# Attention values in float32r: probabilities in two parts, value tiles of 128 stationary columns

## The reference

```python
x = layer_norm(ALPHA * x + 0.5 * swiglu(x, ffn1...))
x = layer_norm(ALPHA * x + hybrid_mixer(x, ...))
x = layer_norm(ALPHA * x + memory_cross_attention(x, mem, ...))
x = layer_norm(ALPHA * x + 0.5 * swiglu(x, ffn2...))
```

```python
o_s = swa_sink_attention(q_s, k_s, v_s, sinks)      # 8 heads of 64, 2 key/value heads, window of 128 keys, a sink per head
o_f = forgetting_attention(q_f, k_f, v_f, f_logit)  # "FoX": 8 heads of 64, causal, with a cumulative forget gate
merged = gates[:, :, 0] * (o_s @ w_branch_swa) + gates[:, :, 1] * (o_f @ w_branch_fox)
return merged @ w_out
```

## Time and profile before

| | |
|---|---|
| median of 3 runs | 1303.44 us (1303.38 to 1303.83) |
| the profiled execution | 1306.2 us, span 1304.4 us |
| PE busy | 1268.3 us, 97% |
| DVE busy | 715.5 us, 55% |
| ACT busy | 449.2 us, 34% |
| POOL busy | 90.4 us, 7% |
| granted TensorE clock | 0.992 of full speed over the span |
| chain that ended last | PE 91%, DVE 3%, POOL 2%, DMA 1%, ACT 1% |

### The profile page before, as it was taken

One profiled execution on the slowest core, in us unless ns is written; L12 is line 12 of the kernel. 1 busy time (PEld: TensorE's weight loads), 2 busy tenths in 40 slices (PEclk: granted clock), 3 DMA queues, 4 the chain that ended last, 5 costly groups with the idle time before them and its releaser, 6 DMA issues.

```text
span 1304.4 us, 16284 instructions
## 1 busy us (share of the span) xinstructions
PE 1268.3 (97%) x6065; PEld 1050.1 (81%) x6065; DVE 715.5 (55%) x994; ACT 449.2 (34%) x699; POOL 90.4 (7%) x126
## 2 busy tenths in 40 slices
PE   7999999999998999999999999999999999999995
PEld 6888888888887887877778887888888888888884
DVE  4644444444475666565644557554664444444446
ACT  3322222222245654455533325342422222222221
POOL 2000000000032100001010030002300000000004
PEclk9999999999999999999999999999999999999998
DMA  7433333333327222222163205213343333333311
GB/s 228 144 96 96 96 96 96 96 96 96 96 66 211 81 82 71 59 56 59 49 209 98 96 33 177 82 49 97 97 129 96 96 96 96 96 96 96 96 48 65
DMA packets 163129, 128.03 MB, mean 98 GB/s; under 512 B 5120, under 2 KB 150544, under 8 KB 163088
## 3 DMA queue, kind: packets, MB, share of 16 engines
q1 hardware_dynamic: 159872, 116.44, 29.8%
q0 software_dynamic: 3008, 11.01, 2.4%
q10 hardware_dynamic: 208, 0.01, 0.0%
HBM read 123.25 MB, written 4.19 MB: 98 GB/s over the span
## 4 chain that ended last, share of the span: by engine, by line
PE 91%; DVE 3%; POOL 2%; DMA 1%; ACT 1%; issue 1%; SPq 0%; DVEq 0%; POOLq 0%; ACTq 0%
PE bank L601 19%; PE bank L603 19%; PE bank L602 19%; PE banks_scores L601 9%; PE banks_scores L603 9%; PE banks_scores L602 9%; PE bank L880 2%; PE bank L862 1%; DVE ring_lo L1406 1%; PE banks_scores L832 1%; PE banks_scores L831 1%; DVE stats L1438 1%; PE bank L619 1%; DMA raw<-in_ffn_w_gate 1%; DVE xT_lo L1406 1%
## 5 line engine op out<-in xcount | busy, mean ns | idle before, releaser
L1406 DVE TENSOR_TENSOR ring_lo<-raw,ring_hi 128x1024 fp32r<-128x1024 f32 x215 | 261.0, 1234 | 123.6 <-ACT ring_hi L1090 123.3
L601 PE MATMUL bank<-xT_hi,ring_hi 128*128 128x512 f32 (+1 forms) x728 | 280.6, 385 | 4.5 <-DVE ring_lo L1406 2.3
L1090 ACT ACTIVATE ring_hi<-raw 128x1024 fp32r<-128x1024 f32 x215 | 221.7, 1056 | 176.5 <-DMA raw<-in_ffn_w_up 89.4
L602 PE MATMUL bank<-xT_lo,ring_hi 128*128 128x512 f32 (+1 forms) x728 | 278.4, 382 | 0.0
L603 PE MATMUL bank<-xT_hi,ring_lo 128*128 128x512 f32 (+1 forms) x728 | 278.3, 382 | 0.0
L601 PEld LDWEIGHTS bank<-xT_hi,ring_hi 128*128 128x128 f32 x728 | 138.8, 191 | 31.0 <-issue 3.9
L603 PEld LDWEIGHTS bank<-xT_hi,ring_lo 128*128 128x128 f32 x728 | 138.7, 191 | 26.3
L602 PEld LDWEIGHTS bank<-xT_lo,ring_hi 128*128 128x128 f32 x728 | 138.9, 191 | 24.9
L601 PE MATMUL banks_scores<-xT_hi,ring_hi 128*128 128x512 f32 (+1 forms) x368 | 140.7, 382 | 0.0
L602 PE MATMUL banks_scores<-xT_lo,ring_hi 128*128 128x512 f32 (+1 forms) x368 | 140.3, 381 | 0.0
L603 PE MATMUL banks_scores<-xT_hi,ring_lo 128*128 128x512 f32 (+1 forms) x368 | 140.3, 381 | 0.0
(11 more groups left out here) (274 smaller groups left out, 1783.0 us busy)
## 6 DMA issues: line engine op xcount, KB each, us to landing
raw<-in_ffn_w_gate SPq DMA_DIRECT2D x44, 512.0 KB, 4.7
raw<-in_ffn_w_up SPq DMA_DIRECT2D x44, 512.0 KB, 4.4
raw<-in_ffn_w_down SPq DMA_DIRECT2D x44, 512.0 KB, 3.3
raw<-in_mix_w_in SPq DMA_DIRECT2D x34, 512.0 KB, 3.8
raw<-in_mem_w_k SPq DMA_DIRECT2D x8, 512.0 KB, 4.1
raw<-in_mix_w_out SPq DMA_DIRECT2D x8, 512.0 KB, 3.2
raw<-in_mem_w_v SPq DMA_DIRECT2D x8, 512.0 KB, 3.2
raw<-in_mem_w_q SPq DMA_DIRECT2D x8, 512.0 KB, 4.7
```

Of the source, the lines that this page charges most:

```text
L601: pe.matmul(dst, hi, mhi, start=start, stop=False)
L602: pe.matmul(dst, hi, mlo, start=False, stop=False)
L1090: nc.scalar.activation(dst, src, copy).then_inc(unit_hi, 1)
L1406: nc.vector.tensor_tensor(dst, src, hi.bitcast(F32), ALU.subtract).then_inc(done, 1)
```

## The change

1. The values product is made of two float32r passes per tile, on the high and on the low part of the transposed probabilities (`probT_hi`, `probT_lo`). The stationary tile holds 128 columns: high and low values side by side. So rows 0 to 63 of bank 7 hold the product with one part of the values and rows 64 to 127 that with the other, and the head's output is the sum of the two halves.
2. ScalarE moves the other half into `o_other` (`output_other`), VectorE adds it to the own half into `os_sum` or `of_sum` (`output_sum`), one head each. The next head's values wait for that sum (`o_added`). The pair's parts are now taken from the sums, at the end of an odd turn.
3. `copied_probs` is done for every bank by both engines: high part by ScalarE, low part by VectorE, and the bank is free after the low part.
4. The tiles of windowed and FoX values are split in the same way (`value_parts_high`, `value_parts_low`), with the order high, low, high for a windowed head and high, low, low, high for a pair of FoX heads, so that either head of a pair finds its own order.
5. From unit 74 (`U_F`) to unit 116 the ring has four slots; two of the six lend their memory to `probT_lo` and to half of the FoX values. `prep(n)` waits for the last user of its slot, unit n - 4. Units 74 and 75 take the slots of 72 and 73.

The diff, cut to its core:

```diff
+MIX_RING = 4
+def slot(n):
+    return (n - U_F) % MIX_RING if U_F <= n < U_OUT else n % RING
+def slot_user(n):
+    for m in range(n - 1, -1, -1):
+        if slot(m) == slot(n):
+            return m
+    return None
...
         def _(pe):
-                if H % 2 == 0 and H >= 2:
-                    pe.wait_ge(o_lo, H // 2)
-                dst = ps[7][HD * (H % 2):HD * (H % 2 + 1), :]
+                if H >= 1:
+                    pe.wait_ge(o_added, H)
                 for k in range(TB):
                     if H < SWA_HEADS:
-                        v = vs[:, k, HD * (H // 4):HD * (H // 4 + 1)]
+                        v = vs_parts[:, k, H // 4, H % 2:H % 2 + 2, :]
...
-                        v = vf[:, k, HD * h:HD * (h + 1)]
+                        v = vf_parts[h // 4][:, k, h // 2 % 2, 2 * (h % 2):2 * (h % 2) + 2, :]
...
-                    mm = pe.matmul(dst[:, P * k:end], v, probT[:, src:src + end - P * k], start=k == 0, stop=k == TB - 1,
+                    pe.matmul(bank(7)[:, P * k:end], v, probT_hi[:, cols], start=k == 0, stop=False, skip_group_check=True)
+                    mm = pe.matmul(bank(7)[:, P * k:end], v, probT_lo[:, cols], start=False, stop=k == TB - 1,
                                    skip_group_check=True)
...
         def _(act):
-                    if n >= RING:
-                        act.wait_ge(unit_used, n - RING + 1)
+                    if slot_user(n) is not None:
+                        act.wait_ge(unit_used, slot_user(n) + 1)
...
             for m in range(4):
+                if m == 1:
+                    value_parts_high(vs_parts, T_VS, ((every, every, every, 0), (every, every, every, 2)))
                 prep(U_QS + m + 4)
...
             def copied_probs(H):
                 for e, n in enumerate(head_uses(H)):
-                    if e != 1:
+                    act.wait_ge(t_full, n + 1)
+                    w = probs_width(H, e)
+                    high(probT_hi[:, HALF * e:HALF * e + w], bank(5 + n % 2)[:, 0:w], probs_hi)
+            def output_other(H):
+                act.wait_ge(o_full, H + 1)
+                if H >= 1:
+                    act.wait_ge(o_added, H)
+                own, other = rows_of(H)
+                nc.scalar.activation(o_other[own, :], ps[7][other, :], copy).then_inc(o_moved, 1)
...
             for H in range(HEADS):
+                if H == SWA_HEADS + 1:
+                    output_other(H - 2)
+                    pair_high((H - 3) // 2)
                 for i, u in enumerate(fill(H % 8)):
-                    if i == 1 and 3 <= H != SWA_HEADS + 1:
-                        pair_high(H - 2)
...
+                if H >= 2 and H != SWA_HEADS + 1:
+                    output_other(H - 2)
                 if H >= 1:
                     copied_probs(H - 1)
-                if H == SWA_HEADS:
-                    pair_high(H - 1)
+                if H < SWA_HEADS:
+                    for u in fill(H):
+                        if u >= 8:
+                            value_parts_high(vf_parts[(u - 8) // 2][:, :, (u - 8) % 2], T_VF[u - 8], ((every, every, slice(0, 4, 3)),))
                 exponentials(...)
                 if H + 1 < HEADS:
                     stack_high(H + 1)
+                if H >= 3 and H % 2 and H != SWA_HEADS + 1:
+                    pair_high((H - 3) // 2)
...
                 if u == 0:
+                    output_other(HEADS - 2)
                     copied_probs(HEADS - 1)
-                    pair_high(HEADS - 1)
+                    output_other(HEADS - 1)
+                    pair_high(HEADS // 2 - 1)
...
         def _(dve):
+            def copied_probs(H, banks=range(2)):
+                for e in banks:
+                    n, w = head_uses(H)[e], probs_width(H, e)
+                    cols = slice(HALF * e, HALF * e + w)
+                    copied[0] += 1
+                    dve.wait_ge(probs_hi, copied[0])
+                    low(probT_lo[:, cols], bank(5 + n % 2)[:, 0:w], probT_hi[:, cols], t_free[n % 2])
+            def output_sum(H):
+                own, _ = rows_of(H)
+                m = H // 2
+                dve.wait_ge(o_moved, H + 1)
+                nc.vector.tensor_tensor((os_sum if m < 4 else of_sum)[own, m % 4, :], ps[7][own, :], o_other[own, :], ALU.add)\
+                    .then_inc(o_added, 1)
```

More of the change, by code:

```diff
@@ L218, in program @@
         qf = place("qf", [P, 4, SEQ], F32, z_q)
-        vf = place("vf", [P, TB, FOX_HEADS * HD], F32, z_v)
+        vf_parts = [place(f"vf_parts{i}", [P, TB, 2, 4, HD], F32R, at) for i, at in enumerate((z_v, z_hi_end))]
         vm_hi = place("vm_hi", [P, MB, D], F32R, z_v)
@@ L1233, in _, with value_parts_high @@
             ins.then_inc(ks_made, 1)
+            def value_parts_high(dst, use, pairs):
+                act.wait_ge(t_full, use + 1)
+                src = turned(5 + use % 2).rearrange("p c (v d) -> p c v d", v=2)
+                for at in pairs:
+                    ins = nc.scalar.activation(dst[at], src, copy)
+                ins.then_inc(v_hi, 1)
+            every = slice(None)
             for m in range(4):
+                if m == 1:
+                    value_parts_high(vs_parts, T_VS, ((every, every, every, 0), (every, every, every, 2)))
                 prep(U_QS + m + 4)
@@ L1255, in exponentials, with pair_high @@
                 ins.then_inc(exp_done, 1)
[L1257 to L1261, removed]
+            def pair_high(m):
+                act.wait_ge(o_added, 2 * m + 2)
+                high((os_hi if m < 4 else of_hi)[:, m % 4, :], (os_sum if m < 4 else of_sum)[:, m % 4, :], o_hi)
             def gate_tanh(n, o, g, m):
@@ L1624, in _, with value_parts_low @@
                                                in1=acc[:, :], op0=ALU.mult, op1=ALU.add).then_inc(c_made, 1)
+            heads_hi = [0]
+            def value_parts_low(lo, hi, use):
+                heads_hi[0] += 1
+                dve.wait_ge(v_hi, heads_hi[0])
+                low(lo, turned(5 + use % 2).rearrange("p c (v d) -> p c v d", v=2), hi, t_free[use % 2])
             split(U_QS + 4)
-            dve.wait_ge(t_full, T_VS + 1)
-            nc.vector.tensor_copy(vs[:, :, :].rearrange("p k c -> p (k c)"), bank(5 + T_VS % 2)).then_inc(t_free[T_VS % 2], 1)
+            value_parts_low(vs_parts[:, :, :, 1, :], vs_parts[:, :, :, 0, :], T_VS)
             for m in range(1, 4):
@@ L1630, in _ @@
                 rotate(qs[:, m - 1, :], O_QS + m - 1)
[L1632 to L1637, removed]
+            copied = [0]
+            def copied_probs(H, banks=range(2)):
[11 more added lines that the diff above has]
+                    .then_inc(o_added, 1)
             def maxima(H, at, sink=None):
@@ L1667, in normalize_probs, with pair_low @@
                 ins.then_inc(p_done, 1)
-            def pair_low(H):
-                m = H // 2
+            def pair_low(m):
                 dve.wait_ge(o_hi, m + 1)
-                hi, lo = (os_hi, os_lo) if m < 4 else (of_hi, of_lo)
-                low(lo[:, m % 4, :], bank(7), hi[:, m % 4, :], o_lo)
+                hi, lo, both = (os_hi, os_lo, os_sum) if m < 4 else (of_hi, of_lo, of_sum)
+                low(lo[:, m % 4, :], both[:, m % 4, :], hi[:, m % 4, :], o_lo)
             def branch_output(n, o, e):
@@ L1704, in _ @@
             for H in range(HEADS):
+                if H == SWA_HEADS + 1:
+                    output_sum(H - 2)
+                    pair_low((H - 3) // 2)
                 for i, u in enumerate(fill(H % 8)):
-                    if i == 1 and 3 <= H != SWA_HEADS + 1:
-                        pair_low(H - 2)
                     n = (U_QF if H < SWA_HEADS else U_G0) + u
@@ L1750, in _ @@
                 if u == 0:
-                    copied_probs(HEADS - 1)
-                    pair_low(HEADS - 1)
+                    output_sum(HEADS - 2)
+                    copied_probs(HEADS - 1, range(3))
+                    output_sum(HEADS - 1)
+                    pair_low(HEADS // 2 - 1)
                 if u % 3 == 2:
```

41 lines of the change are left out of this document (24 added, 17 removed).

## The result

The changed kernel takes 1339.37 us (median of 4 runs, 1335.93 to 1340.59) against 1303.63 us (4 runs): ratio 1.0265, 95% interval 1.024 to 1.0289. It is 35.7 us slower; 1333 had been forecast, within 1315 to 1346. The profiled execution took 1340.21 us with a span of 1338.5, 34.1 us above the span of before.

The account below looks back on a forecast made before the run. Up to the end of the heads, what TensorE issues was taken as the bound. Waits of 28.0, 7.45 and 9.8 us less 15.5 gain made +29.75: 1336 us profiled, 1333 against the runs, within 1315 to 1346.

Parts of the forecast that it names:

- the walk through one turn: Heads: each turn of the loop followed through TensorE, ScalarE and VectorE, lateness carried over; 28.0 us of added waits.
- 12.5 forecast: Heads, to the end of head 15's values: net +12.5 us, 28.0 of waits against 15.5 of gain.
- the gain: Values in the heads: float32r passes take 14.0 us less on TensorE, fewer format changes 1.5; together 15.5 us.
- turn 9: values, branch, third group: Head 9: waits of 1.7 for the last low part, 2.95 for head 7's output, 1.7 at the third transposes.
- The even FoX turns: Heads 10, 12, 14: TensorE waits for the first bank at the third group of transposes, 0.5, 1.2, 1.2 us.
- The term for the changes of format: Eight odd heads: float32r units on both sides of the values, so two format changes go; gain 1.5 us.
- Before the heads: Units 74 and 75, forget gate, first stack: waits of 1.7, 1.8, 1.2 and 2.75 us, together 7.45.
- After the heads: the term that was too small: FoX gate units: preparing unit n+4 waits for the branch's end; TensorE waits 3.25 us three times, 9.8 us.
- VectorE catches up inside each unit: Rival, heads: TensorE's waits vanish under 5.5 us of cover per unit; 1288 us, chance 0.06.
- T+3.04: Odd FoX head: TensorE wants the first bank 3.04 us after T, the start of transposes behind the branch unit.
- Only the ring's waits outside the heads: Rival, no change: only these waits are real, 17.25 us less the 15.5 gain; 1305 us, chance 0.03.
- The products don't get cheaper: Rival, values: each of eight passes loads 128 stationary columns, gain 0 and waits stay; 1349 us, chance 0.05.

Follow-up runs that it names:

- experiment 4: experiment 2 with both queues reordered in the heads: bank copies ahead of the sum of halves, head 7's output earlier; 1294.54 us, ratio 0.9932.
- experiment 1: The kernel before with only the ring of four slots from unit 74 to 116, old values and copies; 1326.91 us, ratio 1.0172.
- Experiment 3: The changed kernel preparing unit n+3 instead of n+4 only in the twelve units after the heads, 105 to 116; 1325.23 us, ratio 1.0168.
- experiment 5: Experiment 3 plus a wait of VectorE for the branch's end ahead of its split of the coming unit; 1338.98 us, ratio 1.026.
- experiment 6: Experiment 3 plus a wait of VectorE for the branch's end behind its split of the coming unit; 1330.42 us, ratio 1.0196.
- experiment 2: The changed kernel preparing unit n+3 instead of n+4 at the place of unit n, in the whole mixer; 1304.13 us, ratio 0.9988.
- experiment 7: The changed kernel, ring and units as they are, with only the queue order of experiment 4; 1330.72 us, ratio 1.0202.

## Why the prediction was right, and where it was short

**The sum of the loss.** Ring's wait alone 23.3 us, the change without that wait 0.5 us, both together 35.7 us. They don't add: 12 us appear only where the ring has moved rounding and split behind the unit's end and a bank also has to pass two engines before it is free. The waits in the heads say the same: 0.2 us listed with the ring alone, 10.9 with the new copies alone, 23.8 with both. This is what the walk through one turn was made for, and it is the step that carried the forecast.

**What was luck in it.** 12.9 us in the heads for 12.5 forecast is three misses that cancel: the waits came out 5.0 us smaller (23.0 for 28.0 beyond the 0.8 of before), the gain about 2 smaller (13.5 for 15.5), and 3.4 us of lower clock had no term at all. Over the whole kernel waits walked too long stand in the same way against a clock that the sum left out.

**Wait by wait** (forecast, then measured in the changed kernel's timeline of TensorE):

| place | forecast | measured |
|---|---|---|
| turns 2 and 4, probabilities | 0.5, 1.75 | 0.2, 1.6 |
| turns 5, 6, 7, value tiles | 1.8, 0.35 + 1.75, 1.95 | 1.9, 0.2 + 1.5, 1.9 |
| turn 8, probabilities and keys | 1.45 | 0.3 + 0.7 |
| turn 9: values, branch, third group | 1.7, 2.95, 1.7 | 1.0, 2.6, 1.5 |
| turns 10, 12, 14, third group | 0.5, 1.2, 1.2 | 0, 0.5, 0.5 |
| turns 11, 13, 15, third group | 2.4 each | 2.2 each |
| unit 105 and the last values | 2.8 | 1.65 + 1.1 |
| **sum of the heads** | **28.8** | **23.8** |

Of the waits forecast only turn 10's 0.5 us is missing, and none stands elsewhere. The even FoX turns are off most for their size (1.0 us for 2.9): in turn 12 VectorE was back 0.7 us earlier than walked.

**The gain.** 15.5 us forecast; the values take 1.21 and 0.89 us for 1.27 and 0.94 forecast, which is 14.9 us for 14.0. The term for the changes of format, 1.5 us, was too large: the first product of the values issues 0.23 us behind the unit instead of 0.32, as taken, but the unit's second product still 0.28 behind its first where it was 0.34, so half of the 0.10 stays. The whole gain, from the heads of experiment 4, is 14.6, or 15.4 with the clock taken out. In the changed kernel's own heads, 23.8 less 0.8 of waits, plus two stretches at the lower clock (unit 105 lasts 7.2 us instead of 5.5, the branch unit of turn 9 the same; 3.4 us together), less the 12.9 measured, leave 13.5; the difference to 15.4 is not accounted for.

**Before the heads.** 1.57 and 1.57 for the two keys' copies (forecast 1.7 and 1.8), 0.96 for the forget gate (1.2), 2.45 for the first stack (2.75): 6.55 for 7.45. The rounding of unit 74 as it was walked, beside the earlier trace rows:

```profile
408.13 1.06 ACT L1120 ACTIVATE ring_hi<-raw 128x1024 fp32r<-128x1024 f32 x1 [4.51 <-PE bank L631]
409.10 0.36 ACT L1217 ACTIVATE km<-bank 128x256 f32<-128x256 f32 x1
```

A wait of 2.33 us on the way, which the kernel before has too, was 0.99 in this execution, so the stretch shows +5.5; in experiment 1, where it was 2.37, it shows +7.15.

**After the heads: the term that was too small.** "0.27 + 1.05 + 1.23 + 0.69 = 3.25, three times, 9.8 us": the waits are 3.28, 3.15 and 3.15, 9.6 us. The term left out was the clock behind them, 8.5 us, in the units behind 105, 107, 110 and 113. It had no row in the trace of before, where no pause of TensorE in the mixer was longer than 0.6 us. Experiment 3 takes pauses and clock away together. Experiments 5 and 6 differ in the length of the pause alone, and the clock falls behind two of three pauses of 2.0 us and none of three of 0.87 us. Length alone doesn't settle it: of the 2.2 us pauses in the changed kernel's heads one of three was followed by a fall, and the pair of 1.1 us waits around unit 105's transposes was followed by one in experiment 2 and by none in experiment 3.

In the trace products issue 0.43 us apart behind each of the three pauses of 3.2 us and 0.23 again later. The Trainium skill (TensorE: Matmul & The Clock Gate, What's actually happening) says that the throttled state is the default and activity releases it. The trace agrees.

The waits come from the order of the queues. In the turn shown nothing behind the rounding of unit n+4 moved before 612.59, although the values whose other half ScalarE moves at 613.67 had been issued by 606.81. The Trainium skill (TensorE: Matmul & The Clock Gate, Architectural detail: the array is 16× 32×32, not 1× 128×128) calls the queues of ScalarE and VectorE strictly first in, first out. The trace agrees.

**The rivals.** "VectorE catches up inside each unit" fails at its own point, the first bank by T+3.04: it came at T+5.36 (617.70 - 612.34). "Only the ring's waits outside the heads" was 17.25 us and is 16.1 plus the clock; experiment 1 shows that as a kernel of its own. "The products don't get cheaper" is out by the rows above.

**What stays open.** Why the ten runs of experiment 2 spread over 7.5 us. The three fastest (1298.72 to 1299.20) had a granted clock of 0.992 to 0.993, the other seven 0.986 to 0.990; as an estimate from these shares that is 4 to 5 us. Why the clock falls behind one pause and not behind another of the same length, and why the wait of 2.3 us before the first scores is 0.99 in some executions, no run here shows.

## What to carry to other kernels

Two buffers given up from a ring of six cost little here (1.1 us, at the output matrix) once the preparation also reached one unit less far: prepare for the slot whose user is done, not for the slot that frees now, since an in-order engine turns that wait into a wait of everything behind it. Here the float32r values are worth about 15 us, and the kernel only shows it (1294.5 us) with one unit less of preparation and with the operations that TensorE wants first standing first in both queues. Before a saving on the bounding engine is booked, walk one turn of the loop on the engines that drain it; a pause costs more than its length when the clock falls behind it.

## What the runs showed of the hardware that had not been expected

After the heads TensorE's clock fell to its lower level (1.2 GHz) at all three pauses of 3.2 us, behind two of three of 2.0 us, and behind none of three of 0.87 us, at distances of 17 to 21 us (granted 0.89, 0.95 and 1.00 over the stretch). The 3.2 us pauses of experiments 1 and 7 repeat it: nine of nine, the fall coming in the pause or at most 1.3 us behind its end. Of the pauses of 2.2 us at a distance of 28 us in the heads only one in three was followed by a fall, in the changed kernel and in experiments 3 and 5 alike. Pauses need not be single: behind unit 105 of experiment 4 a wait of 0.97 us and, 0.4 us after its end, one of 1.29 were followed by a fall. Three pauses, 9.6 us long, cost about 6.4 us more by the clock (12.9 us at half speed); most of the rest of the 18.0 us of the stretch, 1.7, comes from a fall that was there before them, behind unit 105.
